# A hybrid decoder layer on eight cores: bias spread, a resident pair, weight portions and the final norm moved

## The reference

```python
h = rmsnorm(x, g_mix);  proj = h @ w_in
a = proj[..., :512];  z = gelu(proj[..., 512:1536])
gate_a = sigmoid(proj[..., 1536:2560]);  gate_b = sigmoid(proj[..., 2560:])
# pool_mixer: four groups of 128 channels, causal means over 2, 4, 8, 16 tokens minus a, then @ w_pool * s_pool
# spatial_gating: u, v = z's halves; v = rmsnorm(v, g_v); per chunk of 128 tokens u * (tril(w_s) @ v + b_s)
merged = gate_a * (pa @ w_pool_out) + gate_b * (sg @ w_gmlp_out)
x = x + merged @ w_out
h2 = rmsnorm(x, g_ffn)
x = x + (silu(h2 @ w_gate) * (h2 @ w_up)) @ w_down          # 2816 = 22 x 128 features
y = rmsnorm(x, g_final)
```

## Time and profile before

| what | value |
|---|---|
| median of 3 runs | 779.39 us (777.56, 779.39, 871.05) |
| the profiled execution | 779.64 us |
| its span, slowest core (core 3) | 777.8 us |
| spans of cores 0 to 7 | 775.7, 772.7, 775.6, 777.8, 776.2, 773.1, 776.5, 771.6 us |
| TensorE busy, core 3 | 752.4 us, 97% |
| VectorE, ScalarE, GpSimd busy | 533.0 (69%), 370.6 (48%), 106.3 us (14%) |
| granted TensorE clock, by core | 0.990 to 0.997 |

### The profile page before, as it was taken

How to read it: one execution, slowest core, us unless ns; L and a number is a source line. 1 busy time by engine, 2 the same in 40 slices (tenths; PEclk the granted TensorE clock), 3 DMA queues, 4 the chain that set the end, 5 groups by cost and what they waited for, 6 DMA issues and landing times.

```text
span 777.8 us, 14820 instructions; the slowest of 8 cores (771.6 to 777.8 us)
## 1 busy us (share of the span) xinstructions
PE 752.4 (97%) x4868; PEld 442.2 (57%) x4868; DVE 533.0 (69%) x1146; ACT 370.6 (48%) x768; POOL 106.3 (14%) x185
## 2 busy tenths in 40 slices
PE   8999999999999999999999999999999999999995
PEld 3665455666666654445666665434666666654452
DVE  3577659657666666765567766976686665769895
ACT  4588795544444436675444443000554554532222
POOL 3244221001000001110131001002110100001121
PEclk9999999999999999999999999999999999999998
DMA  9998633006213139843499205694942323004652
GB/s 185 218 244 178 126 113 51 7 13 84 42 28 42 29 44 288 159 107 69 67 218 138 42 1 83 222 266 89 169 57 37 54 30 55 1 1 168 213 216 111
DMA packets 47005, 82.92 MB, mean 107 GB/s; under 512 B 20449, under 2 KB 20833, under 8 KB 46914
## 3 DMA queue, kind: packets, MB, share of 16 engines
q0 software_dynamic: 15984, 29.11, 25.9%
q1 hardware_dynamic: 30798, 52.80, 23.3%
q10 hardware_dynamic: 148, 0.07, 0.1%
HBM read 87.83 MB, written 19.49 MB: 138 GB/s over the span
## 4 chain that ended last, share of the span: by engine, by line
PE 82%; ACT 5%; issue 4%; DVE 4%; DMA 3%; POOL 1%; DVEq 0%; ACTq 0%; POOLq 0%; SPq 0%
PE ps L486 80%; ACT junk L507 2%; DVE X L517 2%; DMA Rg<-wpk 2%; ACT Fr L507 1%; PE ps L1262 1%; DMA X<-xd 1%; DVE Fr L517 1%; PE ps L662 1%; POOL rs L634 1%; DMA xd<-X 1%; ACT Sx L507 0%; DVE Pr L517 0%; ACT hT L507 0%; PE ps L1013 0%
## 5 line engine op out<-in xcount | busy, mean ns | idle before, releaser
L507 ACT ACTIVATE Fr<-ps 128x344 f32<-128x344 f32 (+2 forms) x394 | 179.7, 465 | 236.0 <-PE ps L486 224.4
L486 PE MATMUL ps<-hT,Rg 128*128 128x344 f16 x1440 | 247.4, 310 | 4.2 <-ACT Fr L507 3.7
L517 DVE TENSOR_TENSOR Fr<-Fr,ps 128x344 f32<-128x344 f32 (+2 forms) x366 | 179.8, 510 | 95.8 <-ACT Fr L507 69.1
L486 PE MATMUL ps<-Sx,Rg 128*128 128x344 f16 x1080 | 190.0, 310 | 3.0 <-DVE Fr L517 1.6
L486 PEld LDWEIGHTS ps<-hT,Rg 128*128 128x128 f16 x1440 | 140.0, 98 | 78.1 <-issue 8.9
L486 PEld LDWEIGHTS ps<-Sx,Rg 128*128 128x128 f16 x1080 | 104.1, 98 | 59.6 <-issue 9.5
L517 DVE TENSOR_TENSOR X<-X,ps 128x512 f32<-128x512 f32 (+1 forms) x128 | 85.0, 684 | 26.3 <-PE ps L486 21.5
L507 ACT ACTIVATE Fr<-Fr 128x344 f16<-128x344 f32 x138 | 67.2, 487 | 47.3 <-DVE Fr L517 45.7
L486 PE MATMUL ps<-Mr,Pr 128*128 128x512 f16 x352 | 82.1, 379 | 0.2
L547 POOL DMA_DIRECT2D Rg<-wpk x60 | 31.8, 531 | 344.6 <-PE ps L486 343.7
L507 ACT ACTIVATE junk<-X 128x1025 f16<-128x1025 f32 (+1 forms) x41 | 43.4, 1059 | 73.8 <-DVE X L517 68.1
(11 more groups left out here) (116 smaller groups left out, 585.8 us busy)
## 6 DMA issues: line engine op xcount, KB each, us to landing
Rg<-wpk POOLq DMA_DIRECT2D x60, 256.0 KB, 4.4
X<-xp SPq DMA_DIRECT2D x22, 512.0 KB, 7.9
X<-xd SPq DMA_DIRECT2D x20, 512.0 KB, 5.7
Mr<-wpk POOLq DMA_DIRECT2D x34, 256.0 KB, 11.3
yp<-X SPq DMA_DIRECT2D x16, 512.0 KB, 2.9
Pr<-xp SPq DMA_DIRECT2D x10, 512.0 KB, 11.4
xd<-Pr SPq DMA_DIRECT2D x10, 512.0 KB, 6.1
xd<-X SPq DMA_DIRECT2D x10, 512.0 KB, 4.9
```

The source lines that it names most:

```text
L486: ins = e.matmul(out=ap, lhsT=l, rhs=rr, start=(start and i == 0), stop=(stop and i == len(pairs) - 1), skip_group_check=more)
L507: return e.activation(out=P.r(out), in_=P.r(in_), func=func, scale=scale, **kw)
L517: return P.add(eng, lambda e: e.tensor_tensor(out=P.r(out), in0=P.r(a), in1=P.r(b), op=op), reads=[a, b], writes=[out], dur=vdur(n, per), ...
```

## The change

- The row b_s is spread later: behind the load of the last `a` weights, at priority 21 and not -9. g_mix's row is loaded ahead of the first x tile, and fewer dummies are put before 6 us.
- `slots` gets two more rows of Pr. In the first down pass pair 3 (tiles 3 and 11) is reloaded into these, which nothing else then frees or takes.
- The S additions for the first operand of the FFN get a margin of 3.5 us.
- The down weights are asked for later (after unit 19 and 16, not 15 and 9), and each load is gated on one of three successive features' weights and not on one (or none).
- The final norm multiplies by r on ScalarE and by g_final on GpSimd. For the last pair square, multiply and store go by halves of 512, the halves' sums are added by GpSimd, and VectorE multiplies as before.

```diff
@@ -558,7 +558,7 @@
         def U(u):
             return where[u]
 
-        slots = [X[:, i, :] for i in range(NXS + 1)] + [Pr[:, r, :].bitcast(F32) for r in range(10)]
+        slots = [X[:, i, :] for i in range(NXS + 1)] + [Pr[:, r, :].bitcast(F32) for r in range(12)]
         xt_of = {t: t % NXS for t in range(NT)}
         xt_of[NT] = NXS
 
@@ -576,8 +576,8 @@
             x_dma[t] = o_
 
         on = memset('dve', ones[0:1, :], 1.0, -9.0)
+        dma('act', gmix[0:1, :], cst[0:1, C_GMIX:C_GMIX + 1024], 'c1', 4096, -10)
         xload(0, -10.0)
-        dma('act', gmix[0:1, :], cst[0:1, C_GMIX:C_GMIX + 1024], 'c1', 4096, -10)
         dma('act', ident_f[:, :], cst[:, C_ID:C_ID + 128], 'c0', 65536, -9.9)
         dma('act', bs_row[0:1, :], cst[0:1, C_BS:C_BS + 512], 'c4', 4096, -9.8)
         for t in range(1, 4):
@@ -613,13 +613,12 @@
         vcopy(ident_b[:, :], ident_f[:, :], -5, 128)
         act(samT[0:1, 0:8], mhalf[0:1, 0:1].to_broadcast([1, 8]), AF.Square, -9.0, n=8)
 
-        def spread(row, dst, n):
+        def spread(row, dst, n, prio, after=()):
             for c in range(0, n, 512):
                 pt = PT()
-                mm(pt, lambda p: p[:, :], [(ones[0:1, :], row[0:1, c:c + 512])], -9.0)
-                vcopy(dst[:, c:c + 512], PV(pt, lambda p: p[:, :]), -9.0, 512, per=1.04)
-        spread(gmix, gmix, 1024)
-        spread(bs_row, bs_repf, 512)
+                mm(pt, lambda p: p[:, :], [(ones[0:1, :], row[0:1, c:c + 512])], prio, after=after)
+                vcopy(dst[:, c:c + 512], PV(pt, lambda p: p[:, :]), prio, 512, per=1.04)
+        spread(gmix, gmix, 1024, -9.0)
 
         col = [0]
 
@@ -825,6 +824,7 @@
         xl(NT)
         for g in range(4):
             vtt(wsT[:, g, :], ws_raw[:, g, :], mask, ALU.mult, 8.0, 128)
+        spread(bs_row, bs_repf, 512, 21.0, [wd_[('a', 3)]])
         gmix16 = ws_rawf.bitcast(F16)
         vcopy(gmix16, gmix, 35.0, 1024)
         for b in range(4):
@@ -883,11 +883,11 @@
         def blk(j):
             return slice(WJ * j, WJ * (j + 1)), slice(HTOK + WJ * j, HTOK + WJ * (j + 1))
 
-        def ssum(j, prio):
+        def ssum(j, prio, margin=0.0):
             c1, c2 = blk(j)
             A11, A12, A21, A22 = hT[:, 0:4, c1], hT[:, 4:8, c1], hT[:, 0:4, c2], hT[:, 4:8, c2]
             S1, S2, S4 = [Sj[j][:, q, :, :] for q in range(3)]
-            vhh(S1, A21, A22, ALU.add, prio, 4 * WJ)
+            vhh(S1, A21, A22, ALU.add, prio, 4 * WJ, margin)
             vhh(S2, S1, A11, ALU.subtract, prio, 4 * WJ)
             vhh(A21, A11, A21, ALU.subtract, prio, 4 * WJ)
             vhh(S4, A12, S2, ALU.subtract, prio, 4 * WJ)
@@ -1104,13 +1104,14 @@
                     vhh(Pr[:, row, c1], h[0], h[1], ALU.mult, pr, WJ)
             product(a_ops(j), B, False, full, pr, hook)
 
-        def wd_load(nf, fr, prio, after=()):
+        def wd_load(nf, fr, prio, lds):
             hh = nf // 2
             T = [M16[:, nf * 1024 + q * hh * 512:nf * 1024 + (q + 1) * hh * 512].rearrange("p (i c) -> p i c", i=hh)
                  for q in range(3)]
             raw = [M16[:, r * 1024:(r + 1) * 1024] for r in range(nf)]
             B = {n: [] for n in ('B11', 'B21', 'B22', 'T1', 'T2', 'T3', 'T4')}
             for i in range(hh):
+                after = [lds[min(i // 2, 2)]]
                 load(('wd', fr[i]), raw[i], 'd%d' % i, prio + 0.01 * i, after)
                 load(('wd', fr[i + hh]), raw[i + hh], 'd%d' % (i + hh), prio + 0.01 * i, after)
                 B11, B12 = raw[i][:, 0:512], raw[i][:, 512:1024]
@@ -1160,7 +1161,7 @@
                 if tt in keep[0]:
                     keep[0].remove(tt)
                 else:
-                    s_ = xt_of[tt] = freed.pop(0)
+                    s_ = xt_of[tt] = (NXS + 11 + tt // 8) if not last and t == 3 else freed.pop(0)
                     x_dma[tt] = dma('sp', slots[s_][:, 0:D], xd[tt * 128:(tt + 1) * 128, :], 'x%d' % s_, 524288,
                                     prio - 6.0, after=[stored[tt]])
             xa, xb = slots[xt_of[t]], slots[xt_of[t + 8]]
@@ -1175,21 +1176,41 @@
             for tt in (t + 8, t):
                 xv = slots[xt_of[tt]]
                 if last:
-                    final_norm(tt, prio + 1.0)
+                    final_norm(tt, prio + 1.0, t == pair_orders[1][-1])
                 elif hold:
                     keep[1].append(tt)
                 else:
                     stored[tt] = dma('sp', xd[tt * 128:(tt + 1) * 128, :], xv[:, 0:D], 'x%d' % xt_of[tt], 524288, prio + 1.0)
-                if not hold:
+                if not hold and xt_of[tt] <= NXS:
                     freed.append(xt_of[tt])
 
-        def final_norm(t, pr):
+        def final_norm(t, pr, split=False):
             R = 128 if t < NT else NSMP
             xv = slots[xtile(t)][:R, :]
-            r = rstd(xv[:, 0:D + 1], R, 1.0 / 32.0, pr)
-            vstt(xv[:, 0:D], xv[:, 0:D], r, gfin[:R, :], ALU.mult, ALU.mult, pr, D)
             dstd = yp[t * 128:(t + 1) * 128, :] if t < NT else ys[:, :]
-            dma('sp', dstd, xv[:, 0:D], 'o%d' % xtile(t), 524288, pr)
+            if not split:
+                r = rstd(xv[:, 0:D + 1], R, 1.0 / 32.0, pr)
+                act(xv[:, 0:D], xv[:, 0:D], AF.Copy, pr, scale=r, n=D)
+                P.add('pool', lambda e: e.tensor_tensor(out=xv[:, 0:D], in0=xv[:, 0:D], in1=gfin[:R, :], op=ALU.mult),
+                      reads=[xv[:, 0:D], gfin[:R, :]], writes=[xv[:, 0:D]], dur=2000.0, lat=150.0, prio=pr)
+                dma('sp', dstd, xv[:, 0:D], 'o%d' % xtile(t), 524288, pr)
+                return
+            ks = [newcol(), newcol()]
+            for h, c in enumerate((slice(0, 512), slice(512, D + 1))):
+                n = c.stop - c.start
+                act(junk[:R, 0:n], xv[:, c], AF.Square, pr, scale=1.0 / 32.0, accum=ss[:R, ks[h]:ks[h] + 1], n=n)
+            k0, k1 = ks
+            P.add('pool', lambda e: e.tensor_tensor(out=ss[:R, k1:k1 + 1], in0=ss[:R, k0:k0 + 1], in1=ss[:R, k1:k1 + 1],
+                                                    op=ALU.add),
+                  reads=[ss[:R, k0:k0 + 1], ss[:R, k1:k1 + 1]], writes=[ss[:R, k1:k1 + 1]], dur=400.0, lat=100.0, prio=-6.0)
+            P.add('pool', lambda e: e.tensor_tensor(out=rs[:R, k1:k1 + 1], in0=ss[:R, k1:k1 + 1],
+                                                    in1=mhalf[:R, 0:1], op=ALU.pow),
+                  reads=[ss[:R, k1:k1 + 1], mhalf[:R, :]], writes=[rs[:R, k1:k1 + 1]],
+                  dur=560.0, lat=150.0, prio=-6.0)
+            for h in range(2):
+                c = slice(512 * h, 512 * h + 512)
+                vstt(xv[:, c], xv[:, c], rs[:R, k1:k1 + 1], gfin[:R, c], ALU.mult, ALU.mult, pr, 512)
+                dma('sp' if h == 0 else 'act', dstd[:, c], xv[:, c], 'o%d' % (30 + 2 * (t // 8) + h), 262144, pr)
 
         base = 3000.0
         groups = [(0, NFA), (NFA, NF - NFA)]
@@ -1211,7 +1232,7 @@
                         Bf[f] = ffn_load(f, base + 3 * n_)
                 for (f, j) in seqn:
                     if gi == 0 and n_ < 9 and f == part[0]:
-                        ssum(j, 2990.0 + j)
+                        ssum(j, 2990.0 + j, 3500.0)
                     if f not in Bf:
                         Bf[f] = ffn_load(f, base + n_)
                         if gi == 0 and f == 3:
@@ -1219,8 +1240,8 @@
                                 xstore(wo_order[i_], 2990.0 + i_, Bf[f]['ld'])
                     ffn_unit(row(f), j, Bf[f], base + n_)
                     n_ += 1
-                    if n_ == (15 if gi == 0 else 9):
-                        raw, B = wd_load(nf, fr, base + 40.0, [Bf[4]['ld']] if gi == 0 else ())
+                    if n_ == (19 if gi == 0 else 16):
+                        raw, B = wd_load(nf, fr, base + 40.0, [Bf[f_]['ld'] for f_ in ((4, 5, 6) if gi == 0 else (13, 14, 15))])
             base += 100.0
             hh = nf // 2
             if gi == 0:
@@ -1250,7 +1271,7 @@
         for o_ in P.order['pe']:
             if o_.start < 45000.0:
                 gap = o_.start - t_
-                n_ = int((gap - 200.0) / 235.0) if gap > 700.0 else 0
+                n_ = int((gap - 200.0) / (430.0 if t_ < 6000.0 else 235.0)) if gap > 700.0 else 0
                 if n_ > 0:
                     w_ = Op()
                     w_.i = len(P.ops)
```

## The result

The changed kernel takes 796.98 us (median of 6 runs, lowest 796.04) against 780.16 us of the kernel before, measured beside it: ratio 1.0215, 95% interval [1.0186, 1.0244], 17 us slower. The forecast was 777, range 770.5 to 784. Executions in which two or more cores of one die ran at a mean clock of 0.96 or less, as both kernels have at times, are left out of the ratios, though not of the medians.

What follows compares the result with a forecast made beforehand. TensorE was taken as the bound, busy 752.4 of 777.8 us, so gains come only from its holes or end. Terms 1 + 0 - 1.5 - 1.5 + 0 - 0.7 = -2.7 took 779.64 to 777 us, range 770.5 to 784.

Steps and rivals of the forecast that it cites:

- The last pass: Last down pass, final norm moved to ScalarE and GpSimd: 0 us, within -1 and the case of rival 3.
- rival 3: Last pass: GpSimd's multiplies hold VectorE for their whole length, 3.0 us a pair over 6 pairs, +18, 795; chance 0.05.
- the 1.8 us of slack a pair: Last pass: VectorE needs 7.0 us a pair against 8.8 of matmuls, leaving 0.9 us for each GpSimd multiply.
- GpSimd's price: Last pass: a 128 x 1024 multiply taken as 2.4 us, 16 times a 128 x 64 memset of 0.15.
- Rival 4: Last pass: only S operations are held, 1.2 us each, 2.2 a pair: +5, 782; chance 0.12.
- TensorE lost only 1.0 us in 13 there, so little can be gained: Last pass: relieving VectorE of the norm's multiplies gains little; term 0 us.
- Head: Program start: bias cast behind the mask's multiplies delays pool chains and tile 4's multiply; +1 us, bounds -1.5 to +4.
- what is early ahead of that wait only waits longer: Head: gains at the start don't get through, since the u projections wait for their own weights.
- Down weights: FFN groups: loads in portions let the ring's loads share DMA engines with fewer others; -1.5 us, within -4 to +1.
- Fourth pair: First down pass: four resident pairs remove the whole stall at the slot's reload; -1.5 us, bounds -3.6 to 0.
- Tail: Behind the last matmul: norm and stores in halves, end after 8.6 instead of 9.3 us; -0.7, bounds -1.5 to +1.5.

Runs made afterwards that it cites:

- e11: Changed kernel, last pass without PSUM bank 7 but 12 dummy matmuls in that bank ahead of TensorE's waiting group in seven pairs: 792.91 us, 1.0172 of the kernel before.
- e3: Changed kernel with each GpSimd multiply of the final norm cut into four of 256 columns: 772.92 us, 0.9936 of the kernel before.
- e1: Changed kernel with the final norm back on VectorE as one operation, except for the last pair: 775.58 us, 0.9963 of the kernel before.
- e9: As e3, with the head put back as before the change: 770.70 us, 0.9896 of the kernel before.
- e5: As e1, with the head put back as before the change: 773.44 us, 0.9933 of the kernel before.
- e12: As e3, with the bias row spread at priority 7 instead of 21, its cast ahead of the mask's multiplies: 771.41 us, 0.9897 of the kernel before.
- e7: As e5, without the fourth resident pair (pair 3 reloaded into freed slots of X): 772.60 us, 0.9917 of the kernel before.
- e6: As e5, with the down weights asked for as before, nine and twelve loads in a row: 776.89 us, 0.9973 of the kernel before.
- e8: As e5, with the last pair's norm in one piece as before, not halves: 773.12 us, 0.9926 of the kernel before.

## Why the prediction was wrong

- **The last pass, "0, within -1 and the case of rival 3": wrong, and the whole miss.** It cost 20 us. The failed step is the 0 itself: the sum set GpSimd's hold on VectorE at nothing, as if the 1.8 us of slack a pair covered it, and left the hold to rivals with chances of 0.05 and 0.12. The hold is 4.3 us a pair on six cores. GpSimd's price was right, 2.46 us against 2.4, but for a bad reason: a memset of 128 x 1024 takes 0.95 us and not 16 x 0.15. (By the figure of the Trainium skill, "GPSIMD Engine Reference", section 3.1, the estimate was 2.25; the multiplies that meet no S operation take 4.67 / 2 = 2.34.) Rival 4 had the right operations and sized them too small: held "for half a multiply on average, 1.2 us", 2.2 of them in a pair: +5. But the two engines do not meet at random: both follow products of the same pair, and in the rows above multiply and S operation start within 0.2 us of each other, pair after pair. An operation that starts just behind a multiply is held for all of it: 2 x 2.1 = 4.3 us. The other two S operations of a pair run before the multiplies and are free.
- **No term for the clock.** Rivals 3 and 4 price TensorE's loss as the idle alone. The lower clock behind an idle of 2.8 to 3.0 us added at least 1.6 us a pair (e11), and where it fell both S operations were caught in the next pair again, 61 times of 61. A pair takes 13.8 us there, 4.8 more than in e3, in five pairs.
- **Rival 3's number (795) with another mechanism.** It had every operation held, the additions too, which they are not, and was given 0.05. Its hold of 4.8 us a pair is near the measured 4.3, but its 3.0 us of loss over six pairs stands for 4.8 over five on the bad cores. That its 18 us and the measured 17 to 20 agree is luck.
- **"TensorE lost only 1.0 us in 13 there, so little can be gained": too low.** With most of the hold removed, VectorE's relief is worth 0.3 to 0.4% (e3 against e1, with intervals apart; e9 against e5, where they overlap), and core 3 of the changed kernel has 62 matmuls in 754 to 767 where it had 57.
- **Head, +1: right sign, +2.3 measured** (e1 against e5), inside my bounds. The mechanism was another: I looked at tile 4's multiply (forecast 43.6, found 45.15, since the mask's DMA came later), and the cost is a PSUM bank that the spread's product holds until the cast. The step "what is early ahead of that wait only waits longer" held, as e12 shows.
- **Down weights, -1.5: right, undersized.** -3.1 us by time, 24 matmuls by the window. I had scaled it by the one wait at 400; the lost matmuls of the whole window were the better measure.
- **Fourth pair, -1.5: nothing beside the portions.** The stall went, but it is gone in e7 as well, which has the portions alone. That a pair lasts longer than the stall was no proof that the pair would be what removes it; in e6, with the pair and without the portions, the stall is gone too.
- **Tail, -0.7: -0.5 in the trace, nothing measurable in e8.** The chain to the last multiply's end is as long as before (5.9 us behind the last matmul against 5.8), so the gain comes behind it, in the smaller stores.
- The terms without the last pass sum to -2.7; e1, which leaves that one part out, measured -2.9. That they agree is luck in part: terms too high and too low met.

## What to carry over

Before work goes to GpSimd, list the VectorE operations with two SBUF inputs that start at the same time in each round, and count each as held for the whole GpSimd instruction, not for half. If the move is wanted all the same, cut GpSimd's instruction into pieces: the hold was then 0.4 to 0.5 us here. And where a wait of TensorE grows to 3 us, price a fall of the clock behind it: it came on six of eight cores here, and behind none of the waits of 0.8 us. One core out of eight in that state is enough.

## Not expected of the hardware

All eight cores idled 3.0 us in the first pair in which GpSimd multiplied; those whose clock fell behind it took 790 to 795 us, the two whose clock stayed took 777, and in other executions it was other cores. A GpSimd multiply of 128 x 256 took 0.78 us on average, more than a quarter of 2.46, so quarters cost GpSimd a quarter more time, and the kernel still won 2.8%, 22 us, by them.
